# Two-layer hybrid Fourier and mLSTM backbone: both scan directions of a mixer head in flight together

## The reference, cut to what matters

```python
def _bidir_outputs(q, k, v, gates, prev_f, prev_b):
    i_f, f_f, i_b, f_b = gates
    h_f = mlstm_outputs(q, k, v, i_f, f_f, prev_f)
    h_b = mlstm_outputs(_flip(q), _flip(k), _flip(v), _flip(i_b), _flip(f_b), prev_b)
    return h_f + _flip(h_b)
...
    s = jnp.einsum("bhctd,bhcsd->bhcts", qc, kc) * w_intra
    num = (jnp.einsum("bhcts,bhcsd->bhctd", s, vc)
           + w_inter[..., None] * jnp.einsum("bhcde,bhcte->bhctd", c_prev, qc))
    den = jnp.sum(s, axis=-1) + w_inter * jnp.einsum("bhce,bhcte->bhct", n_prev, qc)
    h = num / jnp.maximum(jnp.abs(den), jnp.exp(-m_t))[..., None]
...
    yf = fourier_mix(xf, w_fmix)
    ym = head_norm(h_sum, hn_w).astype(z.dtype) * jax.nn.sigmoid(z)
    return jnp.concatenate([yf, ym], axis=-1) @ w_out
```

## Time and profile before

| | us |
|---|---|
| three runs | 2725.65, 2731.08, 2730.91; median 2730.91 |
| the profiled execution's own time | 2726.1 |
| its span, first to last instruction | 2724.3 |
| TensorE busy in the span | 2546.3 (93%) |
| VectorE busy | 1763.8 (65%) |
| ScalarE busy | 1061.6 (39%) |
| first head stage, from its first projection to the first product with `w_out` | 732.35 to 882.05, 149.70 |
| second head stage, the same | 2132.52 to 2253.08, 120.56 |

### The profile page before, as it was taken

How to read it: one execution, slowest core, us unless ns; L and a number is a source line. 1 busy time by engine, 2 the same in 40 slices (tenths; PEclk the granted TensorE clock), 3 DMA queues, 4 the chain that set the end, 5 groups by cost and what they waited for, 6 DMA issues and landing times.

```text
span 2724.3 us, 33991 instructions
## 1 busy us (share of the span) xinstructions
PE 2546.3 (93%) x13232; PEld 2265.2 (83%) x13232; DVE 1763.8 (65%) x2225; ACT 1061.6 (39%) x1481; POOL 532.6 (20%) x314
## 2 busy tenths in 40 slices
PE   5999999998977999999999999999999887899998
PEld 1999997887966789999888999998887666888877
DVE  2799987675455678888766798775566455522232
ACT  3344433443322454444354544433543424322222
POOL 0154430110200125454011254430111001000001
PEclk9999999999989999999999999999999989899999
DMA  6333336433100243333643433445433102332222
GB/s 236 116 116 117 139 128 242 174 129 97 67 1 0 102 148 114 124 107 132 232 156 137 162 108 131 154 178 203 144 109 97 51 1 93 124 124 92 99 87 77
DMA packets 89068, 330.11 MB, mean 121 GB/s; under 512 B 7424, under 2 KB 23808, under 8 KB 75264
## 3 DMA queue, kind: packets, MB, share of 16 engines
q1 hardware_dynamic: 81680, 312.93, 32.2%
q10 hardware_dynamic: 7280, 15.73, 1.6%
HBM read 320.25 MB, written 8.39 MB: 121 GB/s over the span
## 4 chain that ended last, share of the span: by engine, by line
PE 77%; DVE 13%; issue 5%; ACT 2%; DMA 2%; POOL 0%; SPq 0%; POOLq 0%; DVEq 0%; ACTq 0%
PE ps L1905 26%; PE ps L1865 19%; PE ps L1853 16%; PE ps L857 5%; DVE junk L1524 2%; DVE w_all L1504 2%; DVE w_all L1705 2%; PE ps L963 1%; PE ps L1964 1%; DMA acc<-w_ada_t 1%; PE ps L1954 1%; PE ps L947 1%; PE ps L938 1%; ACT w_all L1209 1%; DVE arena L629 1%
## 5 line engine op out<-in xcount | busy, mean ns | idle before, releaser
L1905 PE MATMUL ps<-w_all,hj_all 128*128 128x512 f32 x2856 | 666.5, 395 | 28.6 <-DVE hj_all L1512 15.7
L1905 PEld LDWEIGHTS ps<-w_all,hj_all 128*128 128x128 f32 x2856 | 541.0, 190 | 145.0 <-DVE w_all L1504 17.8
L1504 DVE TENSOR_TENSOR w_all<-raw,w_all 128x2048 fp32r<-128x2048 f32 x157 | 384.7, 2450 | 302.8 <-ACT w_all L1209 302.6
L1865 PE MATMUL ps<-xn_hi,w_all 128*128 128x384 f32 x1728 | 453.2, 336 | 9.8 <-DVE gate_row L1756 9.6
L1853 PE MATMUL ps<-xn_hi,w_all 128*128 128x384 f32 (+2 forms) x1600 | 433.7, 353 | 21.0 <-DVE arena L1590 9.5
L1209 ACT ACTIVATE w_all<-raw 128x2048 fp32r<-128x2048 f32 x157 | 296.9, 1891 | 277.7 <-PE ps L1905 202.4
L1194 POOL TENSOR_TENSOR x<-x,arena 128x1024 f32<-128x1024 f32 x32 | 79.4, 2501 | 1457.1 <-DVE arena L1590 1457.1
L1524 DVE SCALAR_TENSOR_TENSOR junk<-acc,silu_row 128x1024 bf16<-128x1024 f32 x224 | 326.8, 1459 | 7.8 <-DMA acc<-w_ada_t 3.8
L1853 PEld LDWEIGHTS ps<-xn_hi,w_all 128*128 128x128 f32 x1600 | 293.3, 190 | 44.3 <-issue 16.5
L1865 PEld LDWEIGHTS ps<-xn_hi,w_all 128*128 128x128 f32 x1728 | 313.4, 188 | 15.9 <-DVE gate_row L1756 15.7
L1865 PE MATMUL ps<-xn_lo,w_all 128*128 128x384 f32 x864 | 289.0, 335 | 0.0
(11 more groups left out here) (220 smaller groups left out, 3208.2 us busy)
## 6 DMA issues: line engine op xcount, KB each, us to landing
raw<-w_ff_in SPq DMA_DIRECT2D x104, 1024.0 KB, 4.9
raw<-w_ff_out SPq DMA_DIRECT2D x77, 1024.0 KB, 5.0
acc<-w_ada_t SPq DMA_DIRECT2D x128, 512.0 KB, 3.3
raw<-w_out SPq DMA_DIRECT2D x16, 1024.0 KB, 4.8
raw<-w_in SPq DMA_DIRECT2D x12, 1024.0 KB, 5.3
arena<-w_ada SPq DMA_DIRECT2D x4, 2048.0 KB, 18.6
gate_row<-norm_w ACTq DMA_DIRECT2D x12, 512.0 KB, 6.2
x_out<-x SPq DMA_DIRECT2D x12, 512.0 KB, 9.0
```

Of the source, the lines that this page charges most:

```text
L1504: nc.vector.tensor_tensor(w_lo[par][:, 0:width], raw[par][:, 0:width], w_hi[par][:, 0:width].bitcast(F32), ALU.subtract).then_inc(S["w_lo" ...
L1865: ins = mm(ps[:, bank_, 0:GW], w[:, c], x_[:, k, :], start=start and k == 0 and a == 0, stop=k == 3 and a == 2, skip_group_check=True)
L1905: ins = mm(ps[:, 2 * i + hf, :], xx[:, i * P:(i + 1) * P], w[:, c, hf * 512:(hf + 1) * 512], start=first and c == 0 and a == 0, stop=last ...
```

## The change

`wv`, `wt` and `cst` get a copy for each direction. Each step's PSUM banks are dealt anew: `project` uses 2 and 3, 4 and 5, 2 and 3, 4 and 5 in turn; direction 0 has its maxima and state part in 2 and 3 and its score part in 4 and 5; direction 1 has its maxima and state part in 6 and 7 and its score part in 0 and 1. `outputs` is split into `inter` (state part) and `intra` (score part), `combine` into `gather` (for each direction) and one `combine` for both. TensorE runs the Fourier work of a head between its projections, both directions' `maxima` and `added` follow, and the four output groups come last. The wait on `comb` in the middle of a head is gone; those at the head's start become three waits, each for one pair of banks (`inter_rd` 2k-1, `inter_rd` 2k, `comb` 2k-1), with `comb` 2k ahead of the k by q product. A head's normalisation and gate multiplication run on VectorE inside the next head, and its root on ScalarE ahead of the next head's third projection copy. The arithmetic on tokens is the same.

```diff
@@ -368,13 +368,14 @@
-        wv = head(NT * HV).rearrange("p (t n) -> p t n", t=NT)
-        wt = head(TOK).rearrange("p (t n) -> p t n", t=NT)
-        cst = head(NT * HV).rearrange("p (k n) -> p k n", k=NT)
+        wv = head(2 * NT * HV).rearrange("p (d t n) -> p d t n", d=2, t=NT)
+        wt = head(2 * TOK).rearrange("p (d t n) -> p d t n", d=2, t=NT)
+        cst = head(2 * NT * HV).rearrange("p (d k n) -> p d k n", d=2, k=NT)
...
-        den = small(4 * NT).rearrange("p (a t) -> p a t", a=4)
+        den = head(8 * NT).rearrange("p (a d t) -> p a d t", a=4, d=2)
+        inter_bank, intra_bank, max_bank = (2, 6), (4, 0), (2, 6)
...
@@ -554,7 +555,7 @@

             def project(h, a):

-                dst, b0 = ((qT, 0), (kT, 2), (ktok, 4), (vtok, 0))[a]
+                dst, b0 = ((qT, 2), (kT, 4), (ktok, 2), (vtok, 4))[a]
...
-                if md:
-
-                    act.wait_ge(S["io_mm"], md)
+                if h:
+
+                    act.wait_ge(S["io_mm"], md - 1)
...
+            def deviation(h):
+
+                act.wait_ge(S["hvar"], 4 * m + h + 1)
+                nc.scalar.activation(den[:, 0, 0, 0:n_out], mv[:, 0:n_out, 1], ACT.Sqrt, bias=eps[:, 0:1]).then_inc(S["hstd"], 1)
+
             for h in range(HEADS):
                 k = 4 * m + h
-                for a in range(4):
-                    project(h, a)
-                weights(h, 0)
+                project(h, 0)
                 act.wait_ge(S["ab_mm"], k + 1)
                 take(ab, ps[:, 6, 0:256], 1.0, "ab_sb")
+                project(h, 1)
                 act.wait_ge(S["xab_mm"], k + 1)
...
-                weights(h, 1)
+                if h:
+                    deviation(h - 1)
+                project(h, 2)
+                project(h, 3)
...
                 ins.then_inc(S["f_sb"], 1)
+                weights(h, 0)
                 if h == HEADS - 1:
                     first_out(sub)
-                act.wait_ge(S["hvar"], k + 1)
-                nc.scalar.activation(den[:, 0, 0:n_out], mv[:, 0:n_out, 1], ACT.Sqrt, bias=eps[:, 0:1]).then_inc(S["hstd"], 1)
+                weights(h, 1)
+            deviation(HEADS - 1)
...
-                dve.wait_ge(S["hnT"], mh + 1)
+
+            def mixed(h):
+
+                dve.wait_ge(S["hnT"], 4 * m + h + 1)
                 for g in range(2):
                     w = len(outs[g]) * P
                     mg = mixT[:, g, 4 + h, 0:w]
@@ -823,12 +830,34 @@
                                                          op0=ALU.mult, op1=ALU.mult)
                 ins.then_inc(S["mix_done"], 1)

+            dve.wait_ge(S["w_used"], 2 * (n0 + 7) + START)
+            link(nc.vector.memset(vtok[:, :, HD:HV], 1.0))
+            link(nc.vector.memset(cst[:, :, 0, :], 0.0))
+            dve.wait_ge(S["g_w"], m + 1)
+            for h in range(HEADS):
+                if h:
+                    normed(h - 1)
+                values(h, 0)
+                values(h, 1)
+                if h:
+                    mixed(h - 1)
+                states(h, 0)
+                scores(h, 0)
+                if h == HEADS - 1:
+                    first_out(sub)
+                states(h, 1)
+                scores(h, 1)
+                gather(h, 0)
+                gather(h, 1)
+                combine(h)
+            normed(HEADS - 1)
+            mixed(HEADS - 1)
...
-            pe.wait_ge(S["f_sb"], mh + 1)
...
             def project(h, a):
+
+                k, b0 = 4 * m + h, (2, 4, 2, 4)[a]
+                if a >= 2:
+                    pe.wait_ge(S["qkv_sb"], 4 * k + a - 1)
+                elif h:
...
             def maxima(h, d):

+                k, b0 = 4 * m + h, max_bank[d]
+                if d == 0:
+                    pe.wait_ge(S["qkv_sb"], 4 * k + 3)
+                elif h:
+                    pe.wait_ge(S["mix_done"], k)
+                else:
+                    pe.wait_ge(S["f_sb"], k + 1)
...
+            def likeness(h):
+
+                k = 4 * m + h
+                if h:
+                    pe.wait_ge(S["comb"], 2 * k)
+                pe.wait_ge(S["qkv_sb"], 4 * k + 2)
...
-                pe.wait_ge(S["wv_sb"], 2 * (4 * m + h) + d + 1)
+                md = 2 * (4 * m + h) + d
+                pe.wait_ge(S["wv_sb"], md + 1)
+                if d == 0:
+                    pe.wait_ge(S["qkv_sb"], 2 * md + 4)
+                else:
+                    pe.wait_ge(S["cst_sb"], md)
...
-            def outputs(h, d):
+            def inter(h, d):
+
+
                 md = 2 * (4 * m + h) + d
                 pe.wait_ge(S["cst_sb"], md + 1)
-                pe.wait_ge(S["p_sb"], md + 1)
+                pe.wait_ge(S["wt_sb"], md + 1)
...
+            def intra(h, d):
+
+
+                md = 2 * (4 * m + h) + d
+                pe.wait_ge(S["p_sb"], md + 1)
+                if d == 0:
+                    pe.wait_ge(S["cst_sb"], md + 2)
...
-            def dft_part(tiles, first, last):
...
+            def fold_weights(h):
+
+                k = 4 * m + h
+                if h:
+                    pe.wait_ge(S["inter_rd"], 2 * k)
...
+            def dft(h):
+
+                pe.wait_ge(S["xab_sb"], 4 * m + h + 1)
+                if h == 0:
+                    pe.wait_ge(S["dft_in"], 32 * (m + 1))
...
             def transform(h):

+                pe.wait_ge(S["ab_sb"], 4 * m + h + 1)
+                pe.wait_ge(S["folded"], 4 * m + h + 1)
...
+            pe.wait_ge(S["g_w"], m + 1)
+            pe.wait_ge(S["win_evac"], 12 * m + 12)
             for h in range(HEADS):
                 k = 4 * m + h
-                if h == 0:
-                    pe.wait_ge(S["g_w"], m + 1)
-                    pe.wait_ge(S["win_evac"], 12 * m + 12)
-                else:
-
-                    pe.wait_ge(S["comb"], 2 * k)
                 pe.wait_ge(S["conv_silu"], k + 1)
-                for a in range(3):
-                    project(h, a)
+                project(h, 0)
+                fold_weights(h)
+                project(h, 1)
+                transform(h)
+                project(h, 2)
+                project(h, 3)
+                dft(h)
+                likeness(h)
+                maxima(h, 0)
                 if h:
+                    pe.wait_ge(S["f_sb"], k + 1)
                     head_out(pe, sub, h - 1)
-                pe.wait_ge(S["qkv_sb"], 4 * k + 1)
-                project(h, 3)
-                pe.wait_ge(S["qkv_sb"], 4 * k + 2)
-                maxima(h, 0)
-
-                if h:
-                    pe.wait_ge(S["mix_done"], k)
-                mm(ps[:, 6, 0:P], dft_g[:, 0:P], fmix_w[:, h, :], start=True, stop=True)
-                mm(ps[:, 6, P:2 * P], dft_g[:, P:2 * P], fmix_w[:, h, :], start=True, stop=True).then_inc(S["ab_mm"], 1)
-                pe.wait_ge(S["qkv_sb"], 4 * k + 4)
-                for t in outs[0] + outs[1]:
-                    sl = slice(t * P, (t + 1) * P)
-                    ins = mm(ps[:, t // GT, (t % GT) * P:(t % GT + 1) * P], kT[:, sl], qT[:, sl], start=True, stop=True)
-                ins.then_inc(S["st_mm"], 1)
                 added(h, 0)
-                pe.wait_ge(S["ab_sb"], k + 1)
-                pe.wait_ge(S["folded"], k + 1)
-                transform(h)
-                pe.wait_ge(S["xab_sb"], k + 1)
-                if h == 0:
-                    pe.wait_ge(S["dft_in"], 32 * (m + 1))
-                dft_part([0, 1], True, False)
-                outputs(h, 0)
-
-                pe.wait_ge(S["comb"], 2 * k + 1)
                 maxima(h, 1)
                 added(h, 1)
-                ins = dft_part([2, 3], False, True)
-                if ctx_out:
-                    for t in range(2):
-                        ins = mm(ps[:, 6, 0:CTX], xab[:, NTL + t, :], dft_c[:, t, :], start=(t == 0), stop=(t == 1))
-                ins.then_inc(S["f_mm"], 1)
-                outputs(h, 1)
+                inter(h, 0)
+                intra(h, 0)
+                inter(h, 1)
+                intra(h, 1)

             pe.wait_ge(S["comb"], 2 * HEADS * (m + 1))
```

More of the change, by code:

```diff
@@ L797, in mixer_dve, with combine @@
-            dve.wait_ge(S["g_w"], m + 1)
-            for h in range(HEADS):
-                mh = 4 * m + h
-                for d in range(2):
-                    values(h, d)
-                    states(h, d)
-                    scores(h, d)
-                    if (h, d) == (HEADS - 1, 1):
-                        first_out(sub)
-                    combine(h, d)
+            def combine(h):
+                own.wait()
+                dve.wait_ge(S["comb"], 2 * (4 * m + h) + 2)
+                dn = num[:, :, 0:n_out, HD]
+                link(nc.vector.scalar_tensor_tensor(out=den[:, 1, :, 0:n_out], in0=dn, scalar=-1.0, in1=dn, op0=ALU.mult, op1=ALU.max))
+                link(nc.vector.tensor_tensor(den[:, 2, :, 0:n_out], den[:, 1, :, 0:n_out], em[:, :, 0:n_out, h], ALU.max))
+                link(nc.vector.reciprocal(den[:, 3, :, 0:n_out], den[:, 2, :, 0:n_out]))
```

(20 more changed lines are left out.)

83 lines of the change are left out of this document (42 added, 41 removed).

## The result

The changed kernel takes 2662.05 us (median of 4 runs, 2659.18 to 2662.46) against 2730.56 us (median of 4, 2725.65 to 2731.08). The ratio is 0.9751, with a 95% interval of 0.9734 to 0.9768. The forecast was 2666, in a range of 2657 to 2690. In a second comparison, with five runs against nine of the kernel before, it was 2661.76 against 2727.23, a ratio of 0.9761 (0.9748 to 0.9774).

The account below looks back on a forecast made before the run. The prediction saw latency in the head stages, no engine full, with 43.1 and 36.3 us of waits and low clock. Stages of 112.73 and 93.21 us save 64.3: 2726.1 becomes 2661.8, plus 4.8 gives 2666, range 2657 to 2690.

Parts of the forecast that it names:

- TensorE's floor: Both head stages: TensorE's own unchanged work at 2.4 GHz, 106.57 us of 149.70 and 84.23 of 120.56.
- the sum: TensorE's floor plus remaining waits: stages of 112.73 and 93.21 us, together 64.3 less than before.
- Start of a head at 0: Three bank waits replacing one at a head's start cost nothing; 2.31 us a head would return if their cover went.
- Fourier copies hidden, the 0.96 gone: Between the projections: later projections hide both Fourier copies, so TensorE's wait of 0.96 us a head goes.
- The head before, 2.49 gone and 0.31 in its place: Previous head's normalisation: its 2.49 us wait goes; a 0.31 us wait a head ahead of direction 1's `maxima` comes.
- Banks 4 and 5, 0.83 and 1.28: Direction 0's score part waits for direction 1's states: 0.83 us a head in the first layer, 1.28 in the second.
- The last head, 0.31 and 1.60: First layer's last head: `w_out` copies add 0.31 us, VectorE's reading leaves 1.60 before the first product with `w_out`.
- The clock at no cost: Head stages: granted clock above 0.97, nothing charged; rival, clock stays restless, 2679 to 2691 us, 14%.
- The Trainium skill's rule: Small TensorE idles between PSUM bank groups could keep the clock restless, making the forecast 2691 us instead of 2666.
- The median: Whole run: 4.8 us added to the profiled execution's forecast of 2661.8, giving a median of 2666.
- VectorE's busy time the same within 2 us: Sign of being right: VectorE's busy time in both head stages stays the same within 2 us.

Follow-up runs that it names:

- E4: The changed kernel with one wait more: TensorE waits at a head's start for the last read of the head before; median 2669.60 us.
- e3: The changed kernel with a head's Fourier work back behind its projections, which also moves the root of the head before; median 2692.54 us.
- E7: The changed kernel with a head's square root back at the end of that head on ScalarE, ahead of the next head's first copy; median 2700.69 us.
- e1: The kernel before, with unneeded identity products into an unused PSUM bank ahead of TensorE's three long waits of a head; median 2711.98 us.
- e8: e2 with unneeded identity products into an unused bank at its three long waits in a head; median 2694.38 us.
- e2: The changed kernel with the directions one after the other, direction 0's output groups ahead of direction 1's maxima; median 2719.20 us.

## Why the prediction was right

- **TensorE's floor** (106.57 and 84.23): the total held, its parts less so. In the third head, from start to start, the first two projections with the Fourier weights took 3.03 (the sum had 3.23), `transform` 2.24 (2.30), the other two projections 2.78 (2.68), the transform over tokens 4.30 (4.46), `added` of direction 1 1.19 (1.12) and the score part behind the idle 1.41 (1.34). Together that is 26.64 instead of 26.82.
- **Start of a head at 0:** it held; L958 has no bracket. E4 shows what one common wait would have cost.
- **Fourier copies hidden, the 0.96 gone:** it held, and e3 puts the whole move, with the root's place, at 18.9 and 15.1 us, more than the 0.96 of each head: without it the projections' place has nothing that fits between a product and its copy.
- **The head before, 2.49 gone and 0.31 in its place:** `maxima` 1 starts 1.40 after `added` instead of 1.12, so 0.28. E7 shows that the root's place carries this term.
- **Banks 4 and 5, 0.83 and 1.28:** right in place and cause, but too small. The brackets of 0.80 and 1.25 start at a modelled end; start to start, as the sum counts, the waits are 0.97 and 1.42. The score part starts 0.15 after the end of the states' steps, not 0.05, and the steps start 0.27 after `added` (810.46), not 0.22. The 0.42 for `states` 0 in the second layer was 0.59 by the same count, and 0.12 stands there in the first layer's third head, where the sum had nothing. So the waits were 1.37 instead of 1.14 a head. That a head came out at 28.01 against 27.96 is in part luck: too little wait and too much work cancelled.
- **The last head, 0.31 and 1.60 (second layer 3.72 less 1.75, so 1.97, for both):** this is where the sum was off. The last head was as long as the others up to the end of its output groups (27.93 and 22.87), so VectorE's two copies for `w_out` cost nothing. From the last output group's end to the product with `w_out` it was 1.38 and 1.11. The reading pairs are 1.11 to 1.15 apart, as the sum had them. But they do not run without a break: the last one waits 0.41 and 0.24 for TensorE's last output group, because the score parts come later and take longer than in the sum. Of the 0.45 by which 112.28 is below 112.73 the last head has 0.56, and of the 1.09 in the second layer 0.92; the other heads agree to 0.1.
- **The clock at no cost:** it held at 1.00 in both stages, and e1 shows that the old idles were the cause of the low clock there. The reason that I had given was too simple, though. A low stretch need not follow at once: `added` of direction 1 in the earlier trace rows starts 2.6 us after the idle ends, and the `maxima` in between have a clock of 0.86 (830.92 to 833.54). And an idle of 2.31 need not bring one: L923 in the earlier trace rows runs at 1.00 right after it. So the waits of 0.97 and 1.42 that remain were safe by the runs, not by a limit that the rows had shown.
- **The Trainium skill's rule** that I had weighed, in "TensorE: Matmul & The Clock Gate", section "A second HAM failure mode: psum-queue depth-cycling", did not decide here. E3 has six small waits in a head, in the third five of 0.47 to 1.03 and one of 0.80, and its clock is 0.99 and 1.00. The low stretch in e3's first head, which came with no idle over 1.12, would fit such a rule; it cost 1.6 us and not 25.
- **The median:** the profiled execution was forecast at 2661.8 and took 2662.25. I then added 4.8, since the three runs shown of the kernel before had their median that far above their profiled one. The changed kernel's median has no such distance, and with eight and nine runs the kernel before has 2727.1 and 2727.2. So 4 us of the forecast's error are that step, and 65.5 is the better figure for the gain.
- **What the gain is made of:** the changed kernel's gain in the stages is 65.9, of which 13.2 is clock (e1) and 52.7 are waits. The sum has both in its 64.3, since it was built from lengths at 2.4 GHz.
- **VectorE's busy time the same within 2 us** was wrong: 75.97 to 69.81 and 62.73 to 57.19. The profile's page counts 2187 instructions instead of 2225. The small steps of the division now serve both directions at once, eight clears of `cst` became one a stage, and the paired reads overlap. It was of no weight, as VectorE was not the bound.

At 2.4 GHz the parts can be set side by side. Neither part (e1): 142.7 and 114.3. Directions in series with the Fourier work moved (e8): 131.5 and 106.9. Both directions in flight without the Fourier move (e3): 131.2, of which 1.6 is low clock, and 107.2. Both: 112.3 and 92.1. Each alone gives 11 to 13 and 7, both together 30 and 22. E3 and e8 also carry the moved normalisation, which e1 does not; that part was not tried by itself, so its share is open. The low clock is the other 7 and 6.

## What to carry to other kernels

In a stage where no engine is full, add up one head's work on the engine that ends last and walk its queue against the others once; where that walk met the old trace to 0.2 us, its sums for a new order were within 2.4% of the measured stage wherever the clock stayed full, but for e3 (2.5% and 4%), where one step stood in the wrong place in the walk. Where the sum comes out that well, compare it term by term all the same: here two errors cancelled. Look at what stands behind a waiting instruction on a lightly used engine, as e7 lost 39 us by one call there. And where TensorE has repeated idles of 2 us that can't be removed, products into a free bank, no longer than the idle, are worth a try.

## What the runs showed of the hardware that I had not expected

Filling idles alone took 15 us off the kernel before and 25 off the serial one (2719.20 to 2694.38; the serial kernel's five runs lie between 2711.88 and 2721.02). Idles of 1.22 us at the head borders left the clock at 2.4 GHz in e4, and so did idles of 1.34 in e3's second stage, while three idles a head of 2.05, 1.22 and 2.05 in e2 took it to 0.90 and 0.87. What lies between was not tried. The length of the last idle does not decide by itself: after idles of 2.31 the kernel before ran at 1.00 in one head (806.69 to 809.37) and at 0.61 in another (767.61 to 771.99), and in e3's first head the clock fell to 0.50 for 2.3 us after idles of at most 1.12.
